# Sums of squares of the latent vectors: tile pairs added on Pool, eight narrow products placed between dense matmuls

## What is computed

```python
u = rmsnorm(h, mix_pre_norm[i])
z = u @ w_in[i]
c_q, c_kv, k_r, ml_q, ml_k, ml_v, ml_i, ml_f, ml_o, gates = jnp.split(z, split_idx, axis=-1)
# mla_branch: q = rmsnorm(c_q, q_norm) @ w_uq ; ckv = rmsnorm(c_kv, kv_norm) ; k = ckv @ w_uk ; v = ckv @ w_uv
# mlstm_branch: silu(depthwise_conv(concat([ml_q, ml_k])))
```

## Time and profile before

| | before |
|---|---|
| median of 3 runs | 1271.27 us (1271.18 to 1273.5) |
| the profiled execution's own time | 1272.55 us |
| its span, first to last instruction | 1270.8 us |
| PE busy | 1239.5 us, 98% of the span |
| DVE busy | 669.0 us, 53% |
| ACT busy | 442.0 us, 35% |
| POOL busy | 116.5 us, 9% |
| mean granted TensorE clock | 0.991 of full speed |

### The profile page before, as it was taken

How to read it: one execution, slowest core, us unless ns; L and a number is a source line. 1 busy time by engine, 2 the same in 40 slices (tenths; PEclk the granted TensorE clock), 3 DMA queues, 4 the chain that set the end, 5 groups by cost and what they waited for, 6 DMA issues and landing times.

```text
span 1270.8 us, 15491 instructions
## 1 busy us (share of the span) xinstructions
PE 1239.5 (98%) x5778; PEld 1008.4 (79%) x5778; DVE 669.0 (53%) x1059; ACT 442.0 (35%) x644; POOL 116.5 (9%) x96
## 2 busy tenths in 40 slices
PE   7999999999999999999999999999999999999996
PEld 6888888888887866667888878878888888888875
DVE  5644444442239867667255585584444443222684
ACT  4332333321133436665311523242333332122552
POOL 3000000000024000002011201220000000000343
PEclk9999999999999899999999999999999999999998
DMA  5433233322231331111311123123323323323201
GB/s 194 133 99 99 89 94 98 99 100 99 90 69 50 76 91 52 49 51 54 96 38 47 40 94 116 50 84 115 94 90 96 99 95 103 98 91 109 67 17 67
DMA packets 96865, 107.73 MB, mean 85 GB/s; under 512 B 15062, under 2 KB 87478, under 8 KB 96822
## 3 DMA queue, kind: packets, MB, share of 16 engines
q1 hardware_dynamic: 96608, 107.10, 27.0%
q10 hardware_dynamic: 214, 0.05, 0.0%
HBM read 105.04 MB, written 2.10 MB: 84 GB/s over the span
## 4 chain that ended last, share of the span: by engine, by line
PE 79%; DVE 10%; issue 6%; ACT 3%; POOL 1%; DMA 1%; SPq 0%; DVEq 0%; ACTq 0%; POOLq 0%
PE bank L282 23%; PE bank L284 22%; PE bank L283 22%; DVE v_lo L479 2%; DVE w_lo L312 2%; DVE tbuf L472 1%; PE bank L956 1%; PE bank L383 1%; PE bank L537 1%; PE bank L531 1%; PE bank L532 1%; PE bank L935 1%; PE bank L289 1%; DVE small L1219 1%; PE bank L291 1%
## 5 line engine op out<-in xcount | busy, mean ns | idle before, releaser
L312 DVE TENSOR_TENSOR w_lo<-w_raw,w_hi 128x1024 fp32r<-128x1024 f32 x195 | 243.3, 1253 | 361.9 <-ACT w_hi L305 355.8
L282 PE MATMUL bank<-v_hi,w_hi 128*128 128x512 f32 x904 | 358.7, 397 | 0.0
L284 PE MATMUL bank<-v_hi,w_lo 128*128 128x512 f32 x904 | 353.3, 391 | 0.0
L283 PE MATMUL bank<-v_lo,w_hi 128*128 128x512 f32 x904 | 353.2, 391 | 0.0
L305 ACT ACTIVATE w_hi<-w_raw 128x1024 fp32r<-128x1024 f32 x195 | 203.9, 1055 | 362.1 <-PE bank L284 358.5
L282 PEld LDWEIGHTS bank<-v_hi,w_hi 128*128 128x128 f32 x904 | 170.7, 189 | 36.3 <-issue 2.4
L284 PEld LDWEIGHTS bank<-v_hi,w_lo 128*128 128x128 f32 x904 | 170.5, 189 | 36.3
L283 PEld LDWEIGHTS bank<-v_lo,w_hi 128*128 128x128 f32 x904 | 170.7, 189 | 34.3
L282 PE MATMUL bank<-prod_hi,w_hi 128*128 (+1 forms) x352 | 137.1, 390 | 0.0
L283 PE MATMUL bank<-prod_lo,w_hi 128*128 (+1 forms) x352 | 136.9, 389 | 0.0
L284 PE MATMUL bank<-prod_hi,w_lo 128*128 (+1 forms) x352 | 136.9, 389 | 0.0
(11 more groups left out here) (269 smaller groups left out, 1439.0 us busy)
## 6 DMA issues: line engine op xcount, KB each, us to landing
w_raw<-in_ffn_w_gate SPq DMA_DIRECT2D x44, 512.0 KB, 3.6
w_raw<-in_ffn_w_up SPq DMA_DIRECT2D x44, 512.0 KB, 3.5
w_raw<-in_ffn_w_down SPq DMA_DIRECT2D x44, 512.0 KB, 3.4
w_raw<-in_w_in SPq DMA_DIRECT2D x32, 512.0 KB, 3.6
w_raw<-in_w_out SPq DMA_DIRECT2D x8, 512.0 KB, 3.3
w_raw<-in_ple_w_gate SPq DMA_DIRECT2D x8, 512.0 KB, 3.3
x_tm<-in_x SPq DMA_DIRECT2D x4, 512.0 KB, 7.5
w_raw<-in_w_branch_mla SPq DMA_DIRECT2D x4, 512.0 KB, 3.3
```

The costliest lines, as they stand in the source:

```text
L282: nc.tensor.matmul(o, whi, a_hi, start=start, stop=False)
L283: nc.tensor.matmul(o, whi, a_lo, start=False, stop=False)
L284: return nc.tensor.matmul(o, wlo, a_hi, start=False, stop=stop)
L312: nc.vector.tensor_tensor(w_lo[:, s, :], w_raw[:, s, :], w_hi[:, s, :].bitcast(F32), ALU.subtract).then_inc(w_lo_done, 1)
```

## The change

The four tiles of squares are first added in pairs on POOL: tile 1 onto tile 0, tile 3 onto tile 2 (signal `cq_pair`). On PE, eight single products by the column of ones (instead of sixteen, in pairs that accumulate) are placed inside chunk `MQK + 1`, one behind each of its eight dense groups of three matmuls. `q_sums` is signalled with the last of them, so at the end of chunk `MQK + 1` instead of before it. `bcast_rows` of the inverse roots moves from between `MQK + 2` and `MQK + 3` to behind `MQK + 3`. Nothing changes on DVE, ACT and SP.

```diff
         bs[1].wait(pe, "rb_ready", 1)
         fm_pair(pe, MQK, 0, MQB[0:2], v_hi, v_lo, KD)
-        pe.wait_ge(ms["cq_sq"], 4)
-
-        for g in range(2):
-            for tb in range(TB):
-                for f in range(2):
-                    last = nc.tensor.matmul(B[5][:, 4 * g + tb:4 * g + tb + 1],
-                                            scratch[:, 2 * g + f, tb * P:(tb + 1) * P], ones[:, 0:1],
-                                            start=(f == 0), stop=(f == 1))
+        pe.wait_ge(w_lo_done, MQK + 2)
+        for kk in range(4):
+            for f in range(2):
+                c, i = kk * 256 + f * P, 2 * kk + f
+                last = three(B[MQB[f]][:], wv(MQK + 1, c, c + P), v_hi[:, 4 + kk, :], v_lo[:, 4 + kk, :], False, kk == 3)
+                if i == 7:
+                    last.then_inc(w_used, 1)
+                g, tb = i // 4, i % 4
+                if tb == 0:
+                    pe.wait_ge(ms["cq_pair"], g + 1)
+                last = nc.tensor.matmul(B[5][:, i:i + 1], scratch[:, 2 * g, tb * P:(tb + 1) * P], ones[:, 0:1],
+                                        start=True, stop=True)
         last.then_inc(ms["q_sums"], 1)
-        fm_pair(pe, MQK + 1, 1, MQB[0:2], v_hi, v_lo, KD)
         fm_pair(pe, MQK + 2, 0, MQB[2:4], v_hi, v_lo, KD)
+        fm_pair(pe, MQK + 3, 1, MQB[2:4], v_hi, v_lo, KD)
         pe.wait_ge(ms["rq_ready"], 1)
         bcast_rows(B[6], rq[:, 4:8]).then_inc(ms["rkb_ready"], 1)
-        fm_pair(pe, MQK + 3, 1, MQB[2:4], v_hi, v_lo, KD)
```

```diff
     def mixer_pool(pool):
 
+        for g in range(2):
+            pool.wait_ge(ms["cq_sq"], 2 * g + 2)
+            nc.gpsimd.tensor_tensor(scratch[:, 2 * g, :], scratch[:, 2 * g, :], scratch[:, 2 * g + 1, :],
+                                    ALU.add).then_inc(ms["cq_pair"], 1)
```

## The result

The changed kernel takes 1277.24 us (median of 6, 1275.52 to 1280.59), the kernel before on the same chip 1271.48: slower by a factor of 1.0045, 95% interval 1.0029 to 1.0062, which is 3.7 to 7.9 us. The profiled execution took 1276.40 us (span 1274.6), against 1272.55 (1270.8) before.

A forecast was written before the change was run, and what follows sets the result against it. PE, busy 98% of the span, was taken as the bound. Later sums (3.4), less slack (1.4), plus broadcast (0.9) gave +3.0; slow clock behind the wait added 2.3: +5.3 us, 1276.6, range 1273.8 to 1279.0.

The forecast's parts named there:

- 4 to 6: Sign that the forecast is right: the first query product on PE starts 4 to 6 us later.
- The wait: On PE before chunk MQK + 3: a new wait of 7.4 us on DVE's L312.
- The chain: DVE's gapless work from the sums to the low half of MQK + 3: 12.54 us, moving later with the sums.
- Rival (c): The low half of MQK + 3 is ready when PE arrives, gain kept: -4.4 us, 1266.9; chance 0.04.
- The narrow products: Eight single products inside MQK + 1 on PE: 0.30 us each, 2.4 in all (1.6 to 3.2); sums 3.4 us later.
- The clock in the chunk: PE's granted clock in MQK + 1 with the single products between dense matmuls: taken as 1.00.
- rival (b): Single products drag the clock down inside MQK + 1, 2.3 us more: +7.6 us, 1278.9; chance 0.09.
- The broadcast: Moved behind MQK + 3 it lies on PE's path: 0.81 us start to start and 0.1 in the next matmul.
- The old group: Sixteen narrow products before MQK + 1 on PE cost 6.8 us: 4.4 for the products, 2.4 for the low clock.
- The clock behind the wait: PE's clock falls in the long wait, so dense matmuls behind it start slow: 2.3 us, bounds 0 to 3.1.
- rival (a): The clock holds through PE's wait before MQK + 3: +3.0 us, 1274.3; chance 0.15.
- POOL: Two additions of 1.50 us each cost nothing; two DVE conversions beside them may each be 0.3 us longer, hidden.

The follow-up runs named there:

- late sums: Kernel before, with only q_sums signalled later, three dense matmuls before the end of chunk MQK + 1: 1279.36 us against 1272.60, ratio 1.0050.
- pairs alone: Kernel before with POOL's additions, eight narrow products in one group in the old place: 1271.85 us against 1271.84, ratio 1.0004.
- changed again: The changed kernel run once more, unedited, for a second trace: 1278.26 us against 1272.18 before, ratio 1.0048.
- wait filled: Changed kernel with 30 products of the identity by itself on PE in front of chunk MQK + 3: 1275.34 us, ratio 1.0024 to the kernel before.
- copies late: Kernel before with POOL's additions, eight grouped products, MQK + 3's halves before the waits, wide rotary-key copies before query evictions: 1267.01 us, ratio 0.9958.

## Why the prediction was right

The forecast was +5.3 us to 1276.6; measured were 1277.24 and, by the ratio, +5.7. The mechanism is the one forecast. That the number is so close is in part luck: in the pair of traces the step is only 4.0 us, at the lower edge of the "4 to 6" that was to show the forecast right, since two terms were too large, and the median holds executions in which the clock was lower than in the traced one. Step by step:

- The wait: 7.4 forecast, 7.13 and 7.14 measured, on the instruction named. That it carries the change is shown from both sides: taking DVE's conversion out from behind the sums turns +5.7 into -2.3, and making only the sums late, by more than the change does, gives +6.8.
- The chain: 12.54 us before, 12.5 after. Rival (c) put its sign at about 9.5 us. With the wide copies out of it and the conversion early (and the broadcast in front of MQK + 3), the woven kernel is 4.0 us faster than before, near the -4.4 of that rival.
- The narrow products: I took 0.30 us each. From the first to the last is 430.22 - 423.80, seven steps of 0.917, of which three dense matmuls are 0.68: 0.237 each, 1.9 in all instead of 2.4. The sums were late by 2.9 us then (2.61 in the trace and the 0.25 by which it was ahead), not 3.4. The range of the term held it. The clock in the chunk stayed at 1.00, so rival (b) is out.
- The broadcast: 0.81 from start to start on the path, as forecast. Its removal from there was not measurable beside the clock.
- The old group: I put 4.4 us on the sixteen products and 2.4 on the clock. With the clock up they took 3.49 (423.45 to 426.94 in the kernel with late sums), so 0.9 of the 4.4 was the clock as well. The two together, and so the forecast, stay what they were.
- The clock behind the wait: it fell, so rival (a) is out. I took 2.3; MQK + 3 lost 1.7 in the first trace and 2.9 in the second (7.19 and 8.34 us less 5.45). Together with the smaller lateness, the first trace comes to +4.0 in the stretch to the first query product, and the second (422.53 to 451.78, 29.25) to +5.2. The profiled execution took 1276.40, not the 1277.9 that I gave it. The second execution took 1278.99. The median of the six, 1277.24, lies between the two. Of those without a trace only the mean granted clock is on record: 0.991, as in the traced one, in the three that took 1275.52 to 1278.09, and 0.988 and 0.987 in the two of 1280.15 and 1280.59. Where it fell in them isn't shown.
- POOL: cost nothing here, as forecast, but I had the main victim wrong. The weight conversion beside the first addition took 1.48 us instead of 1.23, near the forecast 0.3. A conversion of a latent tile on DVE (L1166) took 1.83 us instead of 0.745 when it met POOL's second addition, 1.1 us more rather than 0.3, and was covered by the 3.17 us of idle time. In the kernel with pairs alone the cover was gone: DVE came to the sums at 427.8, later than they were ready, and its f_abs was only 0.2 us sooner than before instead of the expected 0.6.

The Trainium skill ("SBUF — State Buffer", section "🔬 SBUF: two separate sides") describes the path that VectorE and GpSimd share as a lock held for a whole instruction, with the other side blocked. The trace agrees roughly: both started at about 422.1, and with the addition's 1.30 us waited out and 0.745 of its own the conversion would have taken 2.04; it took 1.83.

## What to carry to other kernels

Spreading a reduction between dense matmuls makes its result later. Before doing it, follow the result to the engine that waits for it and add up what stands behind that wait, down to the next thing that TensorE needs: here 12.5 us of VectorE work with one weight conversion at its end, against 5.5 us of matmuls to hide it. First take such a conversion out from behind the wait. With that done, both the woven and the grouped form were faster than the kernel before, and without it neither was.

## What the runs showed of the hardware

- An idle stretch on TensorE can be paid twice, as idle time and as slow matmuls behind it. In the wait of 7.1 us the clock fell 3.8 us in, in the second trace 2.8. With 3.16 us idle it fell too, but a microsecond after dense work had started again. A wait of 2.23 us left it alone in the kernel before and in eight more of the twelve traces. In the other three (changed again, wait filled, copies late) the clock fell in that wait or within half a microsecond behind it. One trace in which a wait of two or three microseconds is harmless doesn't show that it always is; I had built the expectation for the pairs alone on that.
- Behind the 7.1 us wait the clock came back 3.5 us after the first dense matmul in one trace and 5.9 us in the other of the same code. At the low level the dense matmuls start 0.43 us apart instead of 0.227, so this alone moves the time by 1.2 us between executions.
- A single product of 128 x 128 float32 weights by one column costs 0.237 us between dense matmuls, about what it costs in a group of four (0.227 in the earlier trace rows), and no less than in the group of eight of the kernel with pairs alone (1.58 us in all, 0.197 each). Dense neighbours made it no cheaper.
- The group of sixteen such products lost the clock 2.5 us after its start in two traces of three, and 4.2 us after it in the third (late sums).
